# A chunked scan's decay sums as products of two rounded parts, with ScalarE making the high part, and three pieces of work in another order

## The reference, cut to what matters

```python
adt = (dt * a).reshape(Bsz, nc, CHUNK, G, J).transpose(0, 1, 3, 4, 2)   # log decays of 16 heads
a_cs = jnp.cumsum(adt, axis=-1)
decay = jnp.exp(segsum(adt))            # segsum: cs[l] - cs[s] for s <= l, else -inf
cb = jnp.einsum('bclgn,bcsgn->bcgls', cc, bc)
y_diag = jnp.einsum('bcgjls,bcsgjp->bclgjp', cb[:, :, :, None] * decay, xg)
decay_to_end = jnp.exp(a_cs[..., -1:] - a_cs)
states = jnp.einsum('bcsgn,bcsgjp->bcgjpn', bc, xg * decay_to_end)
# scan over the 4 chunks: h * chunk_decay + states
y_off = jnp.einsum('bclgn,bcgjpn->bclgjp', cc, prev) * state_decay
```

## Time and profile before

| | |
|---|---|
| median of 3 runs | 1103.57 us (1103.26 to 1104.26) |
| the profiled execution | 1103.89 us, its span 1102.1 us |
| mean granted clock of TensorE | 0.987 of full speed |
| DMA | 123.89 MB, mean 112 GB/s |
| stage with the scan | about 384 to 539 us of the span |
| second layer | from 539 us on |

### The profile page before, as it was taken

The page is one execution under the profiler, slowest core; times in us unless marked ns, Lnnn a source line. Parts: engine busy times, 40 slices in busy tenths (PEclk is TensorE's granted clock), DMA queues, the critical chain, the costliest instruction groups (busy, mean ns, idle before and its releaser), DMA issues. The chain is left out here.

```text
span 1102.1 us, 14438 instructions
## 1 busy us (share of the span) xinstructions
PE 1059.9 (96%) x5558; PEld 872.8 (79%) x5558; DVE 661.8 (60%) x1137; ACT 442.9 (40%) x824; POOL 210.4 (19%) x159
## 2 busy tenths in 40 slices
PE   7999999999999999999899999999999998999997
PEld 4888888888779877788778788887878876888885
DVE  4245435742156597765736865666595667976635
ACT  4223224342266562231623334348623447325432
POOL 0010000000000052201300100002104754045792
PEclk9999999999989999999899999999999999999999
DMA  8276634322041050232324345435221222203401
GB/s 301 78 274 210 220 95 147 114 84 95 8 146 59 3 195 3 74 134 77 125 77 153 115 152 192 153 115 172 78 76 33 103 96 78 77 20 105 183 1 77
DMA packets 58306, 123.89 MB, mean 112 GB/s; under 512 B 5760, under 2 KB 6016, under 8 KB 58112
## 3 DMA queue, kind: packets, MB, share of 16 engines
q1 hardware_dynamic: 55792, 110.22, 29.5%
q0 software_dynamic: 2304, 12.58, 3.2%
q10 hardware_dynamic: 144, 0.20, 0.1%
HBM read 108.83 MB, written 14.16 MB: 112 GB/s over the span
## 5 line engine op out<-in xcount | busy, mean ns | idle before, releaser
L287 DVE TENSOR_TENSOR w_lo<-raw,w_hi 128x2048 fp32r<-128x2048 f32 x58 | 135.6, 2337 | 211.1 <-ACT w_hi L283 200.1
L283 ACT ACTIVATE w_hi<-raw 128x2048 fp32r<-128x2048 f32 x51 | 97.6, 1914 | 211.7 <-PE projections_ps L131 138.3
L129 PE MATMUL projections_ps<-projections_x_hi,w_hi 128*128 128x512 f32 x208 | 81.1, 390 | 0.4 <-ACTq L503 0.4
L131 PE MATMUL projections_ps<-projections_x_hi,w_lo 128*128 128x512 f32 x208 | 81.0, 389 | 0.0
L130 PE MATMUL projections_ps<-projections_x_lo,w_hi 128*128 128x512 f32 x208 | 80.9, 389 | 0.0
L131 PE MATMUL projections_ps<-w_hi,projections_x_lo 128*128 128x512 f32 x192 | 74.7, 389 | 0.0
L130 PE MATMUL projections_ps<-w_lo,projections_x_hi 128*128 128x512 f32 x192 | 74.7, 389 | 0.0
L129 PE MATMUL projections_ps<-w_hi,projections_x_hi 128*128 128x512 f32 x192 | 74.7, 389 | 0.0
L244 DVE SCALAR_TENSOR_TENSOR resid<-resid,mixer_cw 128x512 f32<-128x512 f32 x96 | 64.9, 745 | 0.0
L2428 POOL TENSOR_TENSOR mixer_es<-masks,mixer_gsel 128x1024 f32<-128x1024 f32 x8 | 17.3, 2165 | 230.0 <-PE mixer_ps L1890 152.1
L129 PE MATMUL output_ps<-w_hi,output_m_hi 128*128 128x512 f32 x128 | 53.2, 416 | 0.8 <-DVE output_m_lo L1257 0.7
(11 more groups left out here) (324 smaller groups left out, 2560.5 us busy)
## 6 DMA issues: line engine op xcount, KB each, us to landing
raw<-in_w_in SPq DMA_DIRECT2D x26, 1024.0 KB, 5.0
raw<-in_gdn_w_in SPq DMA_DIRECT2D x24, 1024.0 KB, 5.0
tok<-in_ada_w POOLq DMA_DIRECT2D x16, 768.0 KB, 6.3
raw<-in_w_out SPq DMA_DIRECT2D x8, 1024.0 KB, 5.0
qkv_kept<-mixer_ring SPq DMA_DIRECT2D x8, 1024.0 KB, 4.2
mixer_st<-qkv_kept SPq DMA_DIRECT2D x32, 256.0 KB, 2.9
raw<-in_gdn_w_out SPq DMA_DIRECT2D x8, 1024.0 KB, 5.1
resid<-in_att_bias SPq DMA_DIRECT2D x16, 256.0 KB, 2.6
```

Source lines behind the costliest of these rows:

```text
L129: nc.tensor.matmul(out, w_hi, x_hi, start=first, stop=False, skip_group_check=True)
L131: return nc.tensor.matmul(out, w_lo, x_hi, start=False, stop=last, skip_group_check=True)
L283: self.nc.scalar.activation(self.hi[s][:], self.raw[s][:], ACT.Copy).then_inc(self.hi_ready, 1)
L287: engine.tensor_tensor(self.lo[s][:], self.raw[s][:], self.hi[s][:], ALU.subtract)\
```

## The change

1. **Sums from two parts.** `adt` is split into `adt_parts`: a rounded high part and the rest. `steps_in` holds both, each 128 x 1024 per group, in type fp32r, and `below_r` is the mask in that type. TensorE makes the sums with four fp32r products of 512 columns per step instead of two float32 ones. VectorE makes the parts and `below_r` at the start of the stage (three small instructions).
2. **Who makes the steps.** GpSimd makes the low part (same shape as before). ScalarE makes the high part (`high_steps`), 8 instructions of 128 x 128 per step, one per head, with the head's log decay as the scale.
3. **Order on VectorE.** `rest(0)` comes after the first four `m_lo` and `steps_of(0)`, and `rest(3)` before `outputs(3)`.
4. **Rows of the layer norm.** `row_g` and `row_b` no longer have memory of their own: they lie in `E` and are loaded after the last step's outputs, ahead of the loads of units 6 and 7 in SyncE's queue.
5. **Softplus of the second layer.** `soft_steps.finish`, the betas and `select(0)` come between pair 0 and pair 1 of block 1, instead of after pair 1.

```diff
-        steps_in = sb("steps_in", [P, G, HPG, P])
+        adt_parts = sb("adt_parts", [P, 2, TT, SSM_HEADS], F32R)
+        adt_hi = adt_parts[:, 0].bitcast(F32)
+        steps_in = sb("steps_in", [P, G, 2, HPG, P], F32R)
+        below_r = sb("below_r", [P, P], F32R)
...
-        row_g = sb("row_g", [P, D_MODEL])
-        row_b = sb("row_b", [P, D_MODEL])
+        row_g, row_b = (E[:, n].rearrange("p a b -> p (a b)") for n in range(2))
...  (SyncE)
+            sp.wait_ge(yd_made, STEPS)
+            sp.dma_start(row_g, a["ln_g"].partition_broadcast(P)).then_inc(mod_in, 16)
+            sp.dma_start(row_b, a["ln_b"].partition_broadcast(P)).then_inc(mod_in, 16)
...  (TensorE, ahead_of)
+                pe.wait_ge(steps_hi_ok, s + 1)
...
                 for n in range(2):
-                    mm = nc.tensor.matmul(ps[:, SEG + n, :], below, steps_in[:, g, 4 * n:4 * n + 4, :].rearrange("p a b -> p (a b)"),
-                                          start=True, stop=True)
+                    for part in range(2):
+                        mm = nc.tensor.matmul(ps[:, SEG + n, :], below_r[:],
+                                              steps_in[:, g, part, 4 * n:4 * n + 4, :].rearrange("p a b -> p (a b)"),
+                                              start=part == 0, stop=part == 1)
...  (ScalarE)
+            def high_steps(s):
+
+                c, g = divmod(s, G)
+                if s >= G:
+                    act.wait_ge(seg_made, s - 1)
+                for h in range(HPG):
+                    ins = nc.scalar.activation(steps_in[:, g, 0, h, :], upper, ACT.Copy,
+                                               scale=adt_hi[:, c, g * HPG + h:g * HPG + h + 1])
+                ins.then_inc(steps_hi_ok, 1)
...
+            act.wait_ge(adt_split, 1)
+            high_steps(0)
             round_unit(0)
...
             for e in range(4):
                 high(e)
+            high_steps(1)
             ahead_of(0)
...
             ahead_of(1)
+            high_steps(2)
...
                     round_unit(2)
                     round_unit(3)
+                if s + G < STEPS:
+                    high_steps(s + G)
...  (VectorE)
+            nc.vector.tensor_scalar(adt_parts[:, 0], adt[:], 1.0, None, ALU.mult).then_inc(adt_split, 1)
+            nc.vector.tensor_scalar(below_r[:], below, 1.0, None, ALU.mult).then_inc(adt_split, 1)
+            dve.wait_ge(adt_split, 2)
+            nc.vector.tensor_tensor(adt_parts[:, 1], adt[:], adt_parts[:, 0], ALU.subtract).then_inc(adt_split, 1)
...
-            rest(0)
+            dve.wait_ge(decays_ok, 1)
+            own.did(nc.vector.tensor_tensor(dte[:], dt[:], decays[:, 1], ALU.mult))
             for e in range(4):
                 low(e)
-            dve.wait_ge(decays_ok, 1)
-            own.did(nc.vector.tensor_tensor(dte[:], dt[:], decays[:, 1], ALU.mult))
             own.wait()
+
             steps_of(0)
+            rest(0)
...
-                outputs(s)
                 if s == TT - 1:
                     rest(3)
+                outputs(s)
...  (second layer, VectorE)
                 for pair in range(2):
                     conv.sum_taps(dve, b, pair)
-                if b == 1:
-                    soft_steps.finish(dve).then_inc(g_ok, 1)
+                    if b == 1 and pair == 0:
+
+                        soft_steps.finish(dve).then_inc(g_ok, 1)
...
```

More of the change, by code:

```diff
@@ L915, in scan_and_output @@
         turned, m_hi_ok, m_lo_ok = sem("turned"), sem("m_hi_ok"), sem("m_lo_ok")
+        adt_split, steps_hi_ok = sem("adt_split"), sem("steps_hi_ok")
         steps_ok, seg_made, e_ok = sem("steps_ok"), sem("seg_made"), sem("e_ok")
@@ L954, in _ @@
             sp.dma_start(resid[:], a["x"].rearrange("(t p) d -> p t d", p=P)).then_inc(rows_in, 16)
-            sp.dma_start(row_g[:], a["ln_g"].partition_broadcast(P)).then_inc(rows_in, 16)
-            sp.dma_start(row_b[:], a["ln_b"].partition_broadcast(P)).then_inc(rows_in, 16)
             sp.dma_start(mod_b[:], a["ada_b"]).then_inc(rows_in, 16)
@@ L1106, in _ @@
                 unit_tile(7, t, t, False, True).then_inc(acc_made, 1)
-            pe.wait_ge(mod_in, 16)
+            pe.wait_ge(mod_in, 48)
             pe.wait_ge(added, GROUPS + 1)
@@ L1208, in scan_steps @@
                     pool.wait_ge(seg_made, s - 1)
-                nc.gpsimd.tensor_tensor(steps_in[:, g], upper.unsqueeze(1).broadcast_to([P, HPG, P]),
-                                        adt[:, c, heads_of(g)].unsqueeze(2).broadcast_to([P, HPG, P]), ALU.mult)\
-                    .then_inc(steps_ok, 1)
+                nc.gpsimd.tensor_tensor(steps_in[:, g, 1], upper.unsqueeze(1).broadcast_to([P, HPG, P]),
+                                        adt_parts[:, 1, c, heads_of(g)].unsqueeze(2).broadcast_to([P, HPG, P]),
+                                        ALU.mult).then_inc(steps_ok, 1)
             def skip(s):
@@ L1217, in skip @@
                                         ALU.mult).then_inc(xskip_ok, 1)
+            pool.wait_ge(adt_split, 3)
             scan_steps(0)
@@ L1326, in add_group @@
                     dve.wait_ge(factor_ok, 1)
-                    dve.wait_ge(rows_in, 80)
+                    dve.wait_ge(rows_in, 48)
                 if t < TT - 1:
@@ L1393, in before_factor @@
                 own.did(nc.vector.scalar_tensor_tensor(out=resid[:, t, :], in0=resid[:, t, :],
-                                                       scalar=mean_var[:, t, 0:1], in1=row_g[:],
+                                                       scalar=mean_var[:, t, 0:1], in1=row_g,
                                                        op0=ALU.subtract, op1=ALU.mult))
@@ L1401, in after_factor @@
                 nc.vector.scalar_tensor_tensor(out=resid[:, t, :], in0=resid[:, t, :], scalar=ln_f[:, t:t + 1],
-                                               in1=row_b[:], op0=ALU.mult, op1=ALU.add).then_inc(normed, 1)
+                                               in1=row_b, op0=ALU.mult, op1=ALU.add).then_inc(normed, 1)
+            dve.wait_ge(mod_in, 48)
             step = before_factor(0)
@@ L2577, in _ @@
                     conv.sum_taps(dve, b, pair)
-                if b == 1:
-                    soft_steps.finish(dve).then_inc(g_ok, 1)
-                    dve.wait_ge(beta_step, 1)
-                    nc.vector.tensor_scalar(beta[:], beta[:], 1.0, None, ALU.add).then_inc(beta_step, 1)
-                    dve.wait_ge(beta_step, 2)
-                    nc.vector.reciprocal(beta[:], beta[:]).then_inc(beta_step, 1)
-                    select(0)
+                    if b == 1 and pair == 0:
+                        soft_steps.finish(dve).then_inc(g_ok, 1)
+                        dve.wait_ge(beta_step, 1)
+                        nc.vector.tensor_scalar(beta[:], beta[:], 1.0, None, ALU.add).then_inc(beta_step, 1)
+                        dve.wait_ge(beta_step, 2)
+                        nc.vector.reciprocal(beta[:], beta[:]).then_inc(beta_step, 1)
+                        select(0)
             def select_decays(i):
```

## The result

The changed kernel takes **1113.16 us** (median of 6 runs, 1111.14 to 1115.49) against 1103.84 us (1101.72 to 1104.37, 6 runs): a ratio of 1.0086, 95% interval 1.0074 to 1.0098. It is slower by 9.3 us. The forecast was 1106.3 in a range of 1100.8 to 1109.2, so the direction was right and the size was outside the range.

What follows compares the result with a forecast made beforehand. TensorE's own list of work was taken as the bound, busy 1059.9 of 1102.1 us. The terms -4.9 + 3.6 + 0.3 + 1.3 + 1.9 + 0.5 = +2.7 us gave 1106.3 us, range 1100.8 to 1109.2.

Steps and rivals of the forecast that it cites:

- The sums: Scan steps: four rounded products take 0.92 instead of 1.73 us, 0.81 less per step, 4.9 us gained over steps 2 to 7.
- step 5's sums: Scan, step 5: ScalarE's high steps end at 441.7, TensorE wants them at 441.41; loss 0.3 us (0 to 1.0).
- Eight ScalarE instructions: Scan: the eight new high-step activations of a step take 2.4 us, between 2.0 and 3.1.
- The second part: Start of the scan's stage: the second part of group(0) starts at 405.3 instead of 401.72, loss 3.6 us.
- TensorE's three pauses: Start of the scan's stage: three pauses within 11 us, of about 1.3, 2.7 and 2.4 us.
- Block 1's wait: Second layer, block 1: TensorE's wait for w_lo becomes 4.4 instead of 1.15 us, released by ScalarE's rounding.
- GpSimd's product under pair 1: Second layer, block 1: the selection releases GpSimd early and pair 1 stands still for its product, 1.9 us more (0 to 1.9).
- the clock's term: Start of the scan's stage: a likely fall to 1.2 GHz costs between nothing and 2.7 us, taken as 0.5.
- 1 (GpSimd doesn't disturb pair 1): Block 1: pair 1 and GpSimd don't disturb each other, so 1104.4 us; chance 0.23.
- 2 (GpSimd behind the rests): Scan start: GpSimd goes behind the rests, loss 1.7 instead of 3.6, clock stays up, 1103.9 us; chance 0.22 with combinations.
- 3, the clock's full price: The clock falls in a part that nothing waits behind and costs its full price, 1108.5 us; chance 0.15.
- my own mark: Wrong if PE waits under 3 us in all in the stage's first 25 us, or block 1's wait is gone.

Runs made afterwards that it cites:

- e3: The e2 kernel with select(0) put back behind pair 1, so GpSimd isn't released under it: 1105.64 us, ratio 1.0012.
- e5: The e2 kernel with ScalarE's rounding of the next unit ahead of its last two silu of block 1: 1107.61 us, ratio 1.0039.
- e7: The e2 kernel with both edits, those of e3 and e5: 1105.45 us, ratio 1.0009.
- e8: The e1 kernel plus eight unread products in TensorE's pause ahead of the second part of group(0): 1104.18 us, ratio 1.0009.
- e2: The kernel before with only softplus, betas and selection moved between pair 0 and pair 1 of block 1: 1111.04 us, ratio 1.0069.
- e4: The e2 kernel plus sixteen products of 512 columns, output overwritten, in TensorE's pause of block 1: 1107.94 us, ratio 1.0038.
- e1: The changed kernel with softplus, betas and selection put back behind pair 1, all scan changes kept: 1103.47 us, ratio 0.9997.
- e13: The whole changed kernel, softplus between the pairs, with VectorE's rest(0) moved ahead of the low parts as in e10: 1107.66 us, ratio 1.0035.
- e10: The e1 kernel with VectorE's rest(0) moved ahead of the low parts, ScalarE's order left as changed: 1100.68 us, ratio 0.9964.
- e6: The e1 kernel with the scan start's old order on VectorE and ScalarE, sums still in rounded parts: 1101.32 us, ratio 0.9978.
- e9: The e6 kernel with ScalarE's four squares ahead of step 2's high parts: 1101.34 us, ratio 0.9969.
- e12: The e10 kernel with ScalarE's four squares ahead of step 2's high parts: 1100.61 us, ratio 0.9970.
- e11: The kernel before plus 25 unread products at the place where e2 pauses, nothing moved: 1109.09 us, ratio 1.0040.

## Why the prediction failed

**What held.** The sums: from their start to the second product of the next tile it is 1.24 us (413.08 to 414.32) instead of 1.96, and the products just ahead of them give another 0.08, so a step is 0.8 shorter, as predicted. From the end of `group(0)` on 4.5 us are won, against 4.9 - 0.3 = 4.6 predicted; step 5's sums idle for 0.22 and come some 0.4 late (0.3 predicted). Eight ScalarE instructions take 2.45 (2.4). The second part starts at 405.35, 0.42 of which lie ahead of the stage, so 3.2 late instead of 3.6. TensorE's three pauses there are 2.52, 1.25 and 1.93 where 1.3, 2.7 and 2.4 were expected: the total fits, the split doesn't. Block 1's wait is 4.02 (4.4 predicted, 1.15 before), released by ScalarE's rounding, with GpSimd's product under pair 1: 2.9 us for 1.3 + 1.9. The sum is right and one place in it is not: GpSimd held TENSOR_SCALAR L241, which has one tensor operand and a column, and not L244 as I argued; it cost 1.7 (2.52 against 0.79). e3 and e5 take away one cause each and e7 both: the price is one chain, since 1.92 and 1.43 are left by either alone, and nothing by both.

**The step that failed is the clock's term.** The prediction said: "It costs between nothing ... and 2.7 us ... I take 0.5, near the lower end, since both parts there end in or begin after a wait." The second part of `group(0)` begins after a wait and nothing follows that would absorb it; at half speed it cost 1.5 (4.44 against 2.90 us, and the stage's length in e8). Worse, the term was written for the scan alone. In block 1 I predicted a pause of 4.4 us and gave no price to what the clock does behind it: 1.6 us by e2's rows, and with the fall near 850 some 3 us between e2 and e4. The sum of work and waits, -4.5 + 3.2 + 2.9 with nothing for the clock, is near +1.6; measured is +9.3.

A count over all executions agrees. The span times (1 - mean clock) is what TensorE lacks of full speed, whether or not it had work then, so it is a measure beside the time and not a proof of cause:

```
                 span    clock   span x (1 - clock)   what is left
before          1102.1   0.987        13.8               1088.3
after           1111.3   0.979        23.0               1088.3
e1 (scan)       1101.9   0.986        15.7               1086.2
e2 (softplus)   1109.5   0.984        18.1               1091.4
e13             1106.3   0.984        17.2               1089.1
e10             1099.3   0.989        12.6               1086.6
```

(Means over the runs, each beside its own batch, whose kernel before has 1088.3 to 1088.9 in the last column; a step of 0.001 in a clock is 1.1 us.) What is left moves by -2.1 for the scan and +3.1 for the softplus, within 1 us of the waits and the work (-1.3 and +2.9); the clock's column carries the difference of the whole change.

**Rivals.** 1 (GpSimd doesn't disturb pair 1) is refuted by e3. 2 (GpSimd behind the rests) failed by the rows: its product began 0.43 ahead of the rest. 3, the clock's full price, was the right kind of answer, for one of the three places where the clock cost time in this trace. By my own mark the chain held: PE waits 5.7 us in three pauses of the start.

**What stays open.** Of the 9.3 us, the parts' runs explain 7.3. The other 2 are not clear of noise: the three ratios have intervals of 0.12 to 0.16% to either side, which makes about 2.6 us for their sum. As far as they are real, they go with the mean clock of 0.979, lower than the parts' clocks give; the profiled run was the fastest of the six (0.983), so the places of further falls were not recorded. e13, whose parts add up, speaks against a loss that the two parts make only together, but it has another start than the whole change. Nor is it shown what decides whether a given pause lets the clock fall.

## What to carry to other kernels

A wait that you put in front of TensorE has two prices: its length, and the work behind it at half speed, here 1.5 to 1.7 us per fall, so price both at every new pause of the lengths seen here (1.9 to 4 us), even though two of them, 1.92 in e3 and 1.99 in e6, left the clock up. An engine's instruction order is a resource: one difference of 2.3 us, moved from VectorE's idle time to behind a copy that ScalarE delivers late, gave away 3.5 of the 4.5 us of a good change. And before moving work up on one engine, look at what it releases (GpSimd here) and at what the next engine has queued in front of the result (ScalarE's silu ahead of the rounding).

## What the runs showed of the hardware

The falls do not belong to a piece of code. The small products and short waits near 845 us (0.31, 0.47 and 0.60 us) have 1.00 in the kernel before and in e1, e4, e5, e6, e9, e10 and e12, and fall to 0.50 in the changed kernel and in e2, e3, e7, e8, e11 and e13; e1 and e8 differ only 440 us earlier, and e11 from the kernel before only by products put in. These are single traces; what decides, place in time or chance, is not shown. In the 29 runs of the first batch the kernel before has mean clocks between 0.985 and 0.992, and its spans go from 1106.1 down to 1099.4 with them. At the three places where it could be measured, a fall cost 1.5 to 1.7 us. A gain of 1 us is therefore seen in a stage's length and not in a median over 12 runs.

A GpSimd product that starts 0.17 or 0.18 us behind a VectorE instruction of two SBUF tensors waits for it (3.87 instead of 1.90, in e7 and in the earlier trace rows); where GpSimd is first, VectorE waits: 3.61 and 3.09 instead of 2.29 for the rests, 2.52 instead of 0.79 for a pair of TENSOR_SCALAR, whose second came behind GpSimd's start. The Trainium skill (SBUF — State Buffer, "SBUF: two separate sides") has the port pair as an exclusive lock for a whole instruction; all of these rows agree with it.
